# Latent attention's scores, turns and values by pairs of units instead of single units

## What is computed

```
def attend(args):                       # one block i of 128 queries, 8 heads
    qb, i = args
    s = jnp.einsum('bqhd,bkhd->bhqk', qb, k).astype(jnp.float32)
    q_pos = i * Q_BLOCK + jnp.arange(Q_BLOCK)
    s = jnp.where(k_pos[None, :] <= q_pos[:, None], s, -jnp.inf)
    p = jax.nn.softmax(s, axis=-1).astype(v.dtype)
    return jnp.einsum('bhqk,bkhd->bqhd', p, v)
...
y_b = (mla_attention(...) * jax.nn.silu(mg)) @ w_out_mla[i]
...
gts = jax.nn.sigmoid(gl + gate_bias[i]).reshape(b_, l_, N_BRANCH, D_MODEL)
m = (gts[:, :, 0] * y_a + gts[:, :, 1] * y_b + gts[:, :, 2] * y_c + gts[:, :, 3] * y_d)
```

## Time and profile before

| | us |
|---|---|
| median of 3 runs | 1259.37 |
| lowest and highest of them | 1258.20, 1260.93 |
| the profiled execution | 1258.53 |
| its span (first to last instruction) | 1256.6 |

### The profile page before, as it was taken

How to read it: one execution, slowest core, us unless ns; L and a number is a source line. 1 busy time by engine, 2 the same in 40 slices (tenths; PEclk the granted TensorE clock), 3 DMA queues, 4 the chain that set the end, 5 groups by cost and what they waited for, 6 DMA issues and landing times.

```text
span 1256.6 us, 19833 instructions
## 1 busy us (share of the span) xinstructions
PE 1214.1 (97%) x8349; PEld 993.7 (79%) x8349; DVE 707.3 (56%) x1031; ACT 493.5 (39%) x776; POOL 106.7 (8%) x151
## 2 busy tenths in 40 slices
PE   2899999999999999999999999999999999999998
PEld 2577788789878888888888889798776778888886
DVE  4699878755567543333333467768566555343344
ACT  3443543565246222112222344224465663222232
POOL 4000003621030000000000110000012310000000
PEclk9799999999999999999999999999999999999999
DMA  9665621003023543233222342333222024333311
GB/s 315 208 219 178 210 92 36 3 3 99 7 67 101 168 125 118 76 117 116 86 89 64 106 145 78 101 93 62 68 68 64 16 72 133 94 88 95 114 35 68
DMA packets 150952, 125.58 MB, mean 100 GB/s; under 512 B 16984, under 2 KB 134513, under 8 KB 150736
## 3 DMA queue, kind: packets, MB, share of 16 engines
q1 hardware_dynamic: 147888, 119.88, 31.7%
q10 hardware_dynamic: 1744, 2.36, 0.5%
q0 software_dynamic: 1232, 2.07, 0.5%
HBM read 122.20 MB, written 2.10 MB: 99 GB/s over the span
## 4 chain that ended last, share of the span: by engine, by line
PE 90%; DVE 3%; ACT 2%; DMA 2%; issue 1%; POOL 0%; ACTq 0%; DVEq 0%; POOLq 0%
PE bank L588 56%; PE bank L681 5%; PE bank L830 4%; PE bank L1298 4%; PE bank L1268 4%; PE bank L1332 3%; PE bank L1187 2%; DMA arena<-in_meta_tokens_dram 1%; PE bank L1019 1%; PE bank L1223 1%; PE bank L1240 1%; PE bank L1200 1%; PE bank L639 1%; PE bank L802 1%; PE bank L701 1%
## 5 line engine op out<-in xcount | busy, mean ns | idle before, releaser
L588 PE MATMUL bank<-hsplit,whi 128*128 128x512 f32 (+1 forms) x1872 | 552.1, 379 | 0.8 <-DVE wlo L2054 0.7
L588 PEld LDWEIGHTS bank<-hsplit,whi 128*128 128x128 f32 x1872 | 341.2, 188 | 73.1 <-issue 8.0
L588 PE MATMUL bank<-hsplit,wlo 128*128 128x512 f32 (+1 forms) x936 | 352.2, 376 | 0.0
L2054 DVE TENSOR_TENSOR wlo<-ring,whi 128x2048 fp32r<-128x2048 f32 (+4 forms) x100 | 200.4, 2005 | 180.0 <-ACT whi L1529 179.7
L1529 ACT ACTIVATE whi<-ring 128x2048 fp32r<-128x2048 f32 (+4 forms) x100 | 168.6, 1686 | 133.4 <-DVE xT L2416 53.3
L588 PEld LDWEIGHTS bank<-hsplit,wlo 128*128 128x128 f32 x936 | 175.9, 188 | 32.8
L588 PE MATMUL bank<-a_split,whi 128*128 128x512 f32 x340 | 104.7, 389 | 0.0
L588 PEld LDWEIGHTS bank<-a_split,whi 128*128 128x128 f32 x340 | 63.8, 188 | 13.3
L588 PE MATMUL bank<-a_split,wlo 128*128 128x512 f32 x170 | 66.1, 389 | 0.0
L2083 DVE SCALAR_TENSOR_TENSOR post<-ring,small,post 128x512 f32<-128x512 f32 x77 | 57.9, 752 | 3.7 <-DMA ring<-in_w_ada_dram 1.0
L1470 POOL TENSOR_TENSOR acc<-acc,tb 128x512 f32<-128x512 f32 x12 | 17.7, 1478 | 423.7 <-ACT tb L1766 423.7
(11 more groups left out here) (456 smaller groups left out, 1719.2 us busy)
## 6 DMA issues: line engine op xcount, KB each, us to landing
ring<-in_w_ada_dram SPq DMA_DIRECT2D x24, 1024.0 KB, 5.4
ring<-in_w_in_dram SPq DMA_DIRECT2D x22, 1024.0 KB, 5.3
ring<-in_w_in_dram SPq DMA_DIRECT2D x34, 512.0 KB, 4.8
ring<-in_w_gate_dram SPq DMA_DIRECT2D x11, 1024.0 KB, 5.4
ring<-in_w_up_dram SPq DMA_DIRECT2D x11, 1024.0 KB, 5.4
ring<-in_w_down_dram SPq DMA_DIRECT2D x8, 768.0 KB, 4.6
ring<-in_w_down_dram SPq DMA_DIRECT2D x8, 640.0 KB, 4.2
ring<-in_w_out_dram SPq DMA_DIRECT2D x4, 1024.0 KB, 5.2
```

The lines of the kernel that those rows point to most:

```text
L588: last = mm(o[0:m, 0:n], w[:, k, c0:c0 + m], rhs(s, k), start=k + i == 0, stop=k == kn - 1 and i == 2)
L2054: split_lo = splitter(dve, None, lambda lo, src, hi: tt(lo, src, hi, ALU.subtract))
```

## The change

The loop over 32 units becomes a loop over 16 pairs p = (2p, 2p+1). In one step PE does the turns of both units of pair p-2, the scores of both units of pair p, the values of pair p-3, and then two quarters of a gate tile (twelve matmuls). ACT and DVE get their lists in the same pairs. The remainder of the attention is spread over gate tiles (2,0) and (2,1) instead of (2,0) alone.

```diff
+            def turn_pair(p):
+                for u in (2 * p, 2 * p + 1):
+                    ml_turn(u)
+
+            def values_pair(p):
+                ml_values(2 * p + 1)
+
             mix_quarter(0)
-            for u in range(len(MLU)):
-                ml_scores(u)
-                if u >= 2:
-                    ml_turn(u - 2)
-                for x in ((1,), (2, 3))[u] if u < 2 else (u + 2,):
+            for p in range(MLP):
+                if p >= 2:
+                    turn_pair(p - 2)
+                for u in (2 * p, 2 * p + 1):
+                    ml_scores(u)
+                if p >= 3:
+                    values_pair(p - 3)
+                for x in (2 * p + 2, 2 * p + 3) if p else (1, 2, 3):
                     mix_quarter(x)
-                if u >= 2 and u % 2:
-                    ml_values(u - 2)
-            amid_gl = {1: [(ml_turn, len(MLU) - 2)], 4: [(ml_turn, len(MLU) - 1)], 7: [(ml_values, len(MLU) - 1)]}
+            amid_gl = {(2, 0): {1: [(turn_pair, MLP - 2), (values_pair, MLP - 3)]},
+                       (2, 1): {2: [(turn_pair, MLP - 1), (values_pair, MLP - 2)], 7: [(values_pair, MLP - 1)]}}
...
-                            between=amid_gl if (m, b) == (2, 0) else {})
+                            between=amid_gl.get((m, b), {}))
...
-            for u in range(len(MLU) + 2):
-                if 1 <= u <= len(MLU):
-                    ml_exp(u - 1)
-                if u < len(MLU):
+            for p in range(MLP + 2):
+                for s in range(2):
+                    if 1 <= p <= MLP:
+                        ml_exp(2 * p - 2 + s)
+                    if p >= 2:
+                        ml_copy(2 * p - 4 + s)
+                for u in (2 * p, 2 * p + 1) if p < MLP else ():
                     ml_in(u)
-                if u >= 2:
-                    ml_copy(u - 2)
-                x = u + 2
...
+                for x in (2 * p + 2, 2 * p + 3):
...
             split_hi()
...
+            for p in range(MLP + 2):
+                for s in range(2):
+                    if 1 <= p <= MLP:
+                        ml_rec(2 * p - 2 + s)
+                    if p < MLP:
+                        ml_max(2 * p + s)
+                if p >= 6 and p % 4 == 2 and p < MLP:
+                    ml_gated(p // 4 - 1)
...
+            ml_gated(NB - 1)
             split_lo()
```

More of the change, by code:

```diff
@@ L534, in program @@
         MLU = [(i, h) for i in range(NB) for h in range(8)]
+        MLP = len(MLU) // 2
         keys_of = [META + WIN * (i + 1) for i in range(NB)]
@@ L1958, in gate @@
                 A(dst, bank("gl", m, b)[:, :], func, bias=V1[:, c:c + 1], scale=scale).then_inc(*read("gl", m, b))
-            for u in range(len(MLU) + 2):
-                if 1 <= u <= len(MLU):
-                    ml_exp(u - 1)
-                if u < len(MLU):
-                    ml_in(u)
-                if u >= 2:
-                    ml_copy(u - 2)
-                x = u + 2
[L1968 to L1977, removed]
+            for p in range(MLP + 2):
[5 more added lines that the diff above has]
+                for u in (2 * p, 2 * p + 1) if p < MLP else ():
+                    ml_in(u)
+                for x in (2 * p + 2, 2 * p + 3):
+                    if x >= 4 and x % 4 == 0 and x <= 32:
+                        m, b = MIX_EARLY[x // 4 - 1]
+                        dst, before = early_gate(x // 4 - 1)
+                        if before:
+                            act.wait_ge(*(done("gadd", *before) if before[1] else copied("y", *before)))
+                        gate(dst, m, b, ACT.Tanh, 0.5)
+                    if x in (4, 8, 16, 24):
+                        split_hi(0)
+                    if x in (5, 9, 17, 25):
+                        split_hi(1)
             split_hi()
@@ L2671, in ml_rec @@
                 v.reciprocal(sden[:, c:c + 1], ssumx[:, c:c + 1]).then_inc(*signal("mrec", u))
[L2673 to L2700, removed]
@@ new lines, in ml_gated @@
+            def ml_gated(i):
+                dve.wait_ge(*filled("mo2", i))
+                for pair in range(4):
+                    dve.wait_ge(*copied("mg", pair))
+                y = ybr[:, 2:6, i * WIN:(i + 1) * WIN]
+                tt(y, bank("mo2", i)[:, :].rearrange("p (h t) -> p h t", h=4), y, ALU.mult).then_inc(*read("mo2", i))
+            for p in range(MLP + 2):
[6 more added lines that the diff above has]
+                    ml_gated(p // 4 - 1)
+                for x in (2 * p + 2, 2 * p + 3):
+                    if 4 < x <= 33 and x % 4 == 1:
+                        m, b = MIX_EARLY[x // 4 - 1]
+                        if b != 1:
+                            gate_at, _ = early_gate(x // 4 - 1)
+                            dve.wait_ge(*copied("gl", m, b))
+                            dve.wait_ge(*filled("y", m, b))
+                            gated(mix_sum_of(m) if b == 0 else gate_at, ("y", m, b), gate_at)
+                            if b:
+                                dve.wait_ge(*copied("y", m, b))
+                                tt(mix_sum_of(m), mix_sum_of(m), gate_at, ALU.add).then_inc(*signal("gadd", m, b))
+                    if x in (5, 10, 18, 26):
+                        split_lo(0)
+                    if x in (6, 11, 19, 27):
+                        split_lo(1)
```

## The result

The changed kernel takes 1268.3 us (median of 6 runs, 1267.4 to 1270.2), against 1259.4 us (median of 6, 1258.2 to 1260.9) before. The ratio is 1.0073, with a 95% interval from 1.0061 to 1.0085. The forecast was 1268.7 us, in a range from 1264.8 to 1271.9.

The account below looks back on a forecast made before the run. PE, busy 97% of the span, was taken to set the time; 0 - 1.0 + 0 + 7.7 + 2.6 = +9.3 us on 1259.37 gave 1268.7 us, range 1264.8 to 1271.9.

Parts of the forecast that it names:

- The loop: Attention loop on PE: reordered matmul boundaries cost 0 (-1.3 to +1.4 us); the wait before the last values goes, -1.0 us.
- The low part of the first split: In the loop, DVE's second half of the first weight split, now behind one more unit's maxima: 0, at most 1.1 us.
- The wait for the bank: Behind the loop, PE waits before tile (2,2) for bank 6, until ACT has run tile (2,0)'s gate: +7.7 us.
- The low part of gl21: Behind the loop, DVE's weight part for tile (2,2) ends 3.2 us after the same point, hidden under the 7.7 us.
- The clock: Behind PE's long idle time before tile (2,2), the granted clock falls to 0.50: +2.6 us, bounds 0 to 3.1.
- Rival A: PE waits for the bank before tile (2,2) but the clock stays up: +6.7 us, 1266.1 us; chance 0.11.
- C: Before tile (2,2), PE waits only for gl21's low part, not the bank: +2.2 us, 1261.6 us; chance 0.04 together with E.
- B: The forecast plus new loop boundaries or an early weights wait near their upper bounds: +11.8 us, 1271.2 us; chance 0.15.
- D: Faster: the 0.35 us at each of 16 groups of values vanish, -5.6 us; with C 1256.0 us; chance 0.02.
- E: The values' wait in the loop stays and the tail is no longer: within the noise; chance 0.04 together with C.

Follow-up runs that it names:

- The experiment with the old order: Kernel before the change, values of units 28 and 29 moved from the loop's end behind six matmuls of gate tile (2,0): 1258.5 us.
- the run with both edits: Changed kernel with the gate of tile (2,0) earlier on ACT and the low part of gl21 earlier on DVE: 1258.6 us.

## Why the prediction was right, point by point

**The loop** was taken as 0 for the boundaries and -1.0 for the wait. From the first gate matmul to where PE could go on behind the last `mo2` it was 108.00 us before (1028.62 - 920.62). After, it was 112.52 (1035.75 - 923.23, with 1035.75 as the start of L1231 plus the 0.92 of the earlier trace rows), less the 5.66 of one more gate tile: 106.86. That is -1.1. The boundaries that had no row are in this stretch of the changed kernel:

```profile
942.05 0.38 PE L1201 MATMUL bank<-consts,arena 128*128 128x128 f32 x2
942.27 1.08 PE L1188 MATMUL bank<-arena 128*128 128x272 f32 x4
943.28 0.32 PE L1224 MATMUL bank<-arena 128*64 128x128 f32 x1
...
943.65 0.72 PE L1269 MATMUL bank<-hsplit,whi 128*128 128x512 f32 x2
944.21 0.40 PE L1269 MATMUL bank<-hsplit,wlo 128*128 128x512 f32 x1
```

Scores come 0.22 us behind the start of two transposes (two times 0.11): nothing is lost, as taken. The four records of scores of 272 columns take 1.01 to the start of the values. In the kernel before, two such records with a turn behind them take 0.46:

```profile
942.64 0.62 PE L1187 MATMUL bank<-arena 128*128 128x272 f32 x2
943.10 0.27 PE L1200 MATMUL bank<-consts,arena 128*128 128x128 f32 x1
```

Four are 0.92, so values behind scores cost 0.1, as taken from the gate matmuls. Gate matmuls behind values need 0.56 to the third, again 0.10 too much. One boundary was in no term: in the last query block the second scores of a pair stand behind a matmul of 16 columns and take 0.94 (1014.26 to 1015.20) where the first take 0.86 (1013.26 to 1014.12), at four places 0.3 us, within the bounds. The experiment with the old order confirms the whole: both orders have a stage of 123.7 us once they have no wait.

**The low part of the first split** (bounds 0 to 1.1 us, taken as 0) had its cover: in the changed kernel 7.40 us is the only idle time of PE in the stage, and in the run with both edits there is none.

**The wait for the bank** was summed to 7.7 us, from the rows of ACT. Measured from 1035.75 to 1043.39 it is 7.64. Here the term rested on the order of the code (which bank, and what stands ahead of the gate), which needed no run, and on durations that did not change. The printed order shows how the round comes back to bank 6: between tiles (2,0) and (2,2) banks 7, 0, 1, 2, 4 and 5 are given out, and `mo2` holds 3. Two experiments stand behind the cause: the gate moved ahead takes the wait down to the low part's, and a bank of its own with the low part early takes it away.

**The low part of gl21** was to be hidden, 3.2 us after the same point. It came to 3.3 us after that point in the run with the gate early (1034.89 to 1038.21), of which 3.07 are idle time; the kernel with the old loop and the late tail has the same 3.07.

**The clock** was taken as 2.6 us, from a stretch of 5.64 us at the lower level. It was 5.41 here, and the stage behind the wait, 13.71 us (1043.39 to 1057.10) against 11.12 (1034.28 to 1045.40), is 2.59 longer. The run with added matmuls shows 2.5 by the stage and 2.6 by the medians. That the size agrees so well is luck in part: the stretch was chosen from three, between 3.42 and 6.82 us long, and in the experiments two waits of the same 3.07 us had the fall once inside the wait and once 0.79 us behind it.

**The sum** by the profiles is -1.1 + 7.6 + 2.6 = +9.1 us, the difference of the stages, against +9.3 forecast. That the median came within 0.4 us of the forecast is finer than this method can promise: the runs lie up to 1.9 us from their median, and the profiled execution, forecast at 1267.8, took 1270.2, of which 2.6 us lie ahead of the stage, where both kernels have the same code. The range was written 0.2 us wider than its own terms, whose high ends add up to 1271.7.

Rival A fell with the clock, C with the releaser of the wait and the run with the low part first, B and D with the boundaries, E with the length of the stage. C was also priced too low: the run with the gate early is the case it describes, and its stage is 3.8 us longer than before, not 2.2, since the clock falls for a wait of 3.07 us, too.

## What to carry to other kernels

When banks are handed out in turn, a change in the order of the code also changes which tile must wait for which reader, and a list of the waits with their banks shows that before anything runs; here six tiles and one held bank in between brought the round back to a bank whose reader was late. When the tail of a pipelined loop is moved later, look at what the other engines do only after its end (here ten copies, a table load and a gate) and at the piece of work on the critical engine that used to cover it. Two waits that end at one place have to be removed together: here one edit alone gave 4 us, the other alone nothing, and both 10.

## What I had not expected of the hardware

A wait of 3.07 us was answered by a fall of the clock that began 0.79 us after PE had started again (in the run with the gate early), so the cost stands behind the wait, in rows that show no idle time. It made up a third of the loss of that kernel's tail (1.6 of 4.9 us). The trace of the kernel before has such a case already, right ahead of the stretch of 3.42 us in the earlier trace rows:

```profile
225.17:227.27 2.10, 0.00 (x0) 1.00 0.03 8
227.27:228.76 1.49, 1.49 (x14) 1.00 0.00 0
```

PE is idle for 2.10 us, works for 1.49 us at 1.00, and is then at 0.50 for 3.42 us of work. So neither a clock of 1.00 in the wait nor one of 1.00 just behind it says that the wait was free. No run here tells from which length on a wait costs more than itself: 2.10 us did, among matmuls of 64x64, 1.83 us did not in the one execution that was profiled.

That PE can be kept from this fall by work that nobody needs was expected, and it held: 31 matmuls whose result nobody reads made the kernel 2.6 us faster.
